# First layer's memory attention: transposes two steps behind the scores, eleven steps, first maximum alone ahead of the gate

## The reference, cut to what matters

```python
h = rmsnorm(x, g_mix[0])
mem_k, mem_v = split(rmsnorm(mem, g_mem) @ w_mem_kv[0])     # 256 memory rows, 4 heads of 64
p = h @ w_in_a[0]
u, q_mem = p[..., :2 * 768], p[..., 2 * 768:]
a, gate = split(u + b_glu)
v = causal_dwconv(a * sigmoid(gate), w_dw_a, b_dw_a)        # 768 channels, width 31
mix = silu(layernorm(v))
logits = einsum("bshd,bmhd->bhsm", q_mem, mem_k) / 8        # memory attention
mem_o = einsum("bhsm,bmhd->bshd", softmax(logits), mem_v)
x = x + concatenate([mix, mem_o]) @ w_out[0]
```

## Time and profile before

| | |
|---|---|
| median of 3 runs | 1653.23 us (1648.83 to 1654.64) |
| profiled execution, its own time | 1653.36 us |
| its span, first to last instruction | 1651.6 us |
| granted TensorE clock, mean | 0.996 |
| PE busy | 1605.1 us, 97% |
| DVE busy | 883.3 us, 53% |
| ACT busy | 733.1 us, 44% |
| POOL busy | 714.2 us, 43% |

### The profile page before, as it was taken

How to read it: one execution, slowest core, us unless ns; L and a number is a source line. 1 busy time by engine, 2 the same in 40 slices (tenths; PEclk the granted TensorE clock), 3 DMA queues, 4 the chain that set the end, 5 groups by cost and what they waited for, 6 DMA issues and landing times.

```text
span 1651.6 us, 23637 instructions
## 1 busy us (share of the span) xinstructions
PE 1605.1 (97%) x8452; PEld 1270.7 (77%) x8452; DVE 883.3 (53%) x1451; ACT 733.1 (44%) x1157; POOL 714.2 (43%) x406
## 2 busy tenths in 40 slices
PE   8899999999999999999999999999999999999998
PEld 7656788888888887666888888888887777887776
DVE  7887545445521124434366666611286654587654
ACT  6433544444432235444455555533335643535532
POOL 4433334444445444443444444454435542445431
PEclk9999999999999999999999999999999999999999
DMA  7212133323333332111223233333422443324441
GB/s 255 65 52 65 53 101 102 99 89 91 102 113 102 103 103 71 47 50 39 90 90 102 90 90 100 102 115 112 136 77 81 135 135 109 121 65 131 126 139 51
DMA packets 52972, 161.01 MB, mean 97 GB/s; under 512 B 8736, under 2 KB 8864, under 8 KB 52896
## 3 DMA queue, kind: packets, MB, share of 16 engines
q1 hardware_dynamic: 51744, 156.31, 30.9%
q10 hardware_dynamic: 1152, 3.67, 0.7%
HBM read 141.08 MB, written 2.10 MB: 87 GB/s over the span
## 4 chain that ended last, share of the span: by engine, by line
PE 85%; DVE 10%; ACT 2%; issue 2%; DMA 0%; POOL 0%; DVEq 0%; SPq 0%; ACTq 0%; POOLq 0%
PE banks L1886 23%; PE banks L1888 23%; PE banks L1887 23%; PE banks L2445 2%; PE banks L1932 2%; PE banks L1933 2%; PE banks L1934 2%; PE banks L2161 1%; PE banks L2073 1%; PE banks L2108 1%; DVE roped L1678 1%; PE banks L2091 1%; DVE chain L1497 1%; DVE pt_c L1724 1%; PE banks L2068 1%
## 5 line engine op out<-in xcount | busy, mean ns | idle before, releaser
L651 POOL TENSOR_TENSOR w_lo<-raw,w_hi 128x1024 fp32r<-128x1024 f32 x252 | 610.1, 2430 | 700.4 <-ACT w_hi L734 700.2
L1886 PE MATMUL banks<-xs_hi,w_hi 128*128 128x512 f32 (+2 forms) x1488 | 590.7, 397 | 5.1 <-DVE xs_lo L1559 1.6
L1888 PE MATMUL banks<-xs_hi,w_lo 128*128 128x512 f32 (+2 forms) x1488 | 577.5, 388 | 0.0
L1887 PE MATMUL banks<-xs_lo,w_hi 128*128 128x512 f32 (+2 forms) x1488 | 576.6, 388 | 0.0
L734 ACT ACTIVATE w_hi<-raw 128x1024 fp32r<-128x1024 f32 x255 | 263.8, 1052 | 235.8 <-PE banks L1888 204.6
L1886 PEld LDWEIGHTS banks<-xs_hi,w_hi 128*128 128x128 f32 x1488 | 280.2, 188 | 74.4 <-issue 19.0
L1888 PEld LDWEIGHTS banks<-xs_hi,w_lo 128*128 128x128 f32 x1488 | 280.0, 188 | 57.8
L1887 PEld LDWEIGHTS banks<-xs_lo,w_hi 128*128 128x128 f32 x1488 | 280.6, 189 | 52.3 <-issue 0.5
L1886 PE MATMUL banks<-hid_hi,w_hi 128*128 128x512 f32 x352 | 136.9, 389 | 0.0
L1887 PE MATMUL banks<-hid_lo,w_hi 128*128 128x512 f32 x352 | 136.9, 389 | 0.0
L1888 PE MATMUL banks<-hid_hi,w_lo 128*128 128x512 f32 x352 | 136.9, 389 | 0.0
(11 more groups left out here) (273 smaller groups left out, 2018.9 us busy)
## 6 DMA issues: line engine op xcount, KB each, us to landing
raw<-wstream SPq DMA_DIRECT2D x255, 512.0 KB, 3.5
swap_c<-prob_c SPq DMA_DIRECT2D x256, 64.0 KB, 2.0
x<-xT SPq DMA_DIRECT2D x4, 512.0 KB, 9.7
out<-pt SPq DMA_DIRECT2D x8, 256.0 KB, 2.0
memx<-memT SPq DMA_DIRECT2D x4, 256.0 KB, 5.1
ws_sb<-wsT ACTq DMA_DIRECT2D x2, 512.0 KB, 4.6
rope_sb<-rope ACTq DMA_DIRECT2D x2, 512.0 KB, 6.1
qk<-post_rows ACTq DMA_DIRECT2D x2, 512.0 KB, 5.0
```

The source lines that it names most:

```text
L651: nc.gpsimd.tensor_tensor(w_lo[s][:].rearrange("p k c -> p (k c)"), raw[s][:], w_hi[s][:].rearrange("p k c -> p (k c)").bitcast(f32), SUB) ...
L1886: MM(dst, w_hi[slot][:, k, :], hi, start=start, stop=False)
L1887: MM(dst, w_hi[slot][:, k, :], lo, start=False, stop=False)
L1888: return MM(dst, w_lo[slot][:, k, :], hi, start=False, stop=stop)
```

## The change

The table gets eleven steps in place of ten: (2,0), (2,3), (2,7), (3,3), (3,7), (4,3), (4,7), (5,3), (5,7), (6,3), (6,7). At step i PE issues the scores of block i and the transposes of block i-2, DVE and ACT copy block i-2 down. The outputs stand at steps 6 and 10. Ahead of the gate product DVE now issues only the maximum and the reciprocal of block 0; all other maxima and reciprocals stand in their steps. `pair_ended` is no longer called. No instruction is added or dropped; the second output stays at (6,7).

```diff
--- before.py
+++ after.py
@@ -72,7 +72,7 @@
 IN2_UNITS = DFF // P
 ATT_FIRST = 9
 STEP = 6
-A_AT = [divmod(16 + 39 * i // 9, KT) for i in range(10)]
+A_AT = [divmod(16 + 39 * i // 10, KT) for i in range(11)]
 B_AT = [(3 + i, 4) for i in range(8)]
 B_AT += [divmod(11 * KT + 40 * p // 3 + q, KT) for p in range(MT) for q in (0, 3, 6, 10)]
 B_LATE = 7
@@ -932,8 +932,8 @@
                     for i in a_steps(j, k):
                         if 0 < i < att_m0.n:
                             exponentials(att_m0, i)
-                        if 1 <= i <= att_m0.n:
-                            odd_down(att_m0, i - 1)
+                        if 2 <= i <= att_m0.n + 1:
+                            odd_down(att_m0, i - 2)
             gate_sigmoid(MT - 1)
             high_for(U_MEM1)
             for p in range(2):
@@ -1506,32 +1506,25 @@
 
             for j in range(2 * MT):
                 t = j // 2 - 1
-                ahead = a_steps(j, 0) + a_steps(j, 1) if j in (2, 4) else []
-                for i in ahead:
-                    maxima(att_m0, i)
-                    if i == 0:
-                        inverses(att_m0, 0)
-                        maxima(att_m0, 1)
-                        even_down(att_m0, 0)
+                if j == 2:
+                    maxima(att_m0, 0)
+                    inverses(att_m0, 0)
                 if j >= 2 and j % 2 == 0:
                     own.wait()
                     glu_product(t)
                 for k in range(KT):
                     at = KT * (j % 2) + k
                     for i in a_steps(j, k):
-                        if 1 < i < att_m0.n and i not in ahead:
+                        if 0 < i < att_m0.n:
                             maxima(att_m0, i)
-                        if 1 < i <= att_m0.n:
-                            even_down(att_m0, i - 1)
-                        if 1 < i < att_m0.n:
+                        if 2 <= i <= att_m0.n + 1:
+                            even_down(att_m0, i - 2)
+                        if 0 < i < att_m0.n:
                             inverses(att_m0, i)
-                        p = pair_ended(i)
-                        if p is not None:
-                            mem_out_down(p)
+                        if i in (QT + 2, 2 * QT + 2):
+                            mem_out_down(i // QT - 1)
                     if t >= 0:
                         conv_taps(t, at, at + 1)
-                    if (j, k) == (2, 2):
-                        inverses(att_m0, 1)
                 if 8 <= j < 12:
                     conv_finish(j - 8)
                 scaled(glu[:, j // 2, CW - 1:] if j % 2 == 0 else gate[j // 2 % 2][:], U_GLU + j,
@@ -2206,13 +2199,12 @@
                     if i == 0:
                         pe.wait_ge(acc_free, U_GLU)
                     scores(att_m0, i)
-                p = pair_ended(i)
-                if p is not None:
-                    output(att_m0, p)
-                if i == 1:
+                if i in (QT + 2, 2 * QT + 2):
+                    output(att_m0, i // QT - 1)
+                if i == 2:
                     pe.wait_ge(vt_down, VT_M0 + 2)
-                if 1 <= i <= att_m0.n:
-                    transposes(att_m0, i - 1)
+                if 2 <= i <= att_m0.n + 1:
+                    transposes(att_m0, i - 2)
 
             def ln_rows(dst, src, tiles):
 
```

## The result

The changed kernel takes 1660.38 us in the median of 5 runs (1658.22 to 1661.25), the kernel before 1653.23 (1648.83 to 1654.64, 5 runs). The ratio is 1.0042, with a 95% interval of 1.0029 to 1.0054: slower by about 7 us, and between 5 and 9. The profiled execution took 1659.49, its span is 1657.7 (before: 1653.36 and 1651.6).

The account below looks back on a forecast made before the run. DVE's path through the attention was taken as the bound up to its last copy, which lets `conv_parts` start. Terms summed to 5.06 us later, 1653.36 to 1658.4 us; full range 1654.5 to 1661.0, the forecast's own 1656.5 to 1660.3.

Parts of the forecast that it names:

- (a): First gate product and block 1: product starts only 0.17 earlier, block 1 then needs a whole uncovered step, +1.60 us.
- (c): Second gate product: with step 4 ahead of it, DVE waits for ACT's chain up to the sigmoid, +2.64 us.
- (d): POOL's low parts of the weights hold DVE taps with two SBUF inputs: units 3, 4, 5 cost +0.33, +0.04, +0.44 us.
- (e): From unit 5 on: one copy more stands alone, +0.34 us; the third gate product waits less, -0.33 us.
- Does DVE wait for PE after the change?: Tightest at block 6: PE's scores, output and transposes, 3.1 us, against DVE's 3.25 ahead of its copy; no wait, 0.
- Rival 1: PE's waits in the attention stretch decide, those for scaled probabilities go: faster, 1650.8 us; chance 0.10.
- Rival 2: ACT is ready for the second sigmoid, so that product costs 0 to 0.9: 1655.8 to 1656.7 us; chance 0.14.
- rival 3: POOL's low parts meet other DVE taps: 1655.2 us if only `banks`, 1660.1 if both whole; chance 0.12.
- Rival 4: The end hangs on something other than DVE's last copy and stays: 1653.4 us; chance 0.04.

Follow-up runs that it names:

- e1_gate2: Changed kernel with step 4 back at (4,1) and block 4's maximum ahead of the second gate product: ratio 1.0039, first maximum to `conv_parts` 55.32 us.
- e2_head: Changed kernel with block 1's maximum back ahead of the first gate product, its reciprocal behind tap 2: ratio 1.0022, first maximum to `conv_parts` 56.30 us.
- e4_busy: Changed kernel plus twelve PE products that nobody reads, ahead of block 6's scores: ratio 1.0033, first maximum to `conv_parts` 55.66 us.
- e8_both_busy: e3_both plus sixteen PE products that nobody reads, ahead of block 5's scores: first maximum to `conv_parts` 52.02 us, single execution.
- e10_swap4: Changed kernel with ACT's sigmoid ahead of the weights' high part in unit 4: first maximum to `conv_parts` 58.65 us, single execution.
- e5_lag: Kernel before with only the lag of two, its own early places and maxima kept, two late steps: ratio 1.0007, first maximum to `conv_parts` 54.66 us.
- e6_cover: Kernel before with DVE's convolution tap moved between copy and reciprocal from block 2 on: ratio 1.0007, first maximum to `conv_parts` 49.58 us.
- e7_lag_cover: Kernel before with only the lag of two, and DVE's tap moved ahead of the reciprocal: ratio 1.0001, first maximum to `conv_parts` 52.56 us.
- e3_both: Changed kernel with early maxima of blocks 1 and 4 back and step 4 at (4,1): ratio 1.0021, first maximum to `conv_parts` 53.53 us.
- e11_busy2: Changed kernel plus unread PE products, nine ahead of block 2's scores and twelve ahead of block 6's: first maximum to `conv_parts` 55.70 us, single execution.

## Why the prediction was right, and where not

The time, 1660.38, is in the range (1654.5 to 1661.0), at its upper end, and just above the forecast's own (1656.5 to 1660.3). The direction was right.

| step | forecast | profile after |
|---|---|---|
| (a) block 1's step (55.98 - 47.73, against 54.87 - 48.25) | +1.60 | +1.63 |
| (c) second gate product (75.96 - 70.85 = 5.11, against 2.45) | +2.64 | +2.66 |
| (d) low part of unit 3: 62.38 to 64.84 less a tap 0.66, against 1.49 | +0.33 | +0.31 |
| (d) low part of unit 4: product 76.89 - 75.96, against 0.78 | +0.04 | +0.15 |
| (d) low part of unit 5: 1.26, against 0.88 | +0.44 | +0.38 |
| (e) one copy alone | +0.34 | +0.34 |
| (e) third gate product | -0.33 | -0.34 |
| DVE's wait for PE at block 4's copy (86.48 - 83.11, against 1.85) | 0 | **+1.52** |
| sum | 5.06 | 6.65 |
| last copy less first maximum (56.32, against 49.64) | | 6.68 |

(a) and (c) are shown by taking them back: the wait of 2.58 goes to 0.26 in `e1_gate2`, the one of 1.09 goes in `e2_head`. What each would give the stretch alone can't be read from these two, as PE's waits and the clock moved with each edit. Both together can be, from the two runs in which the clock costs DVE nothing (the second a single execution): 55.66 in `e4_busy` less 52.02 in `e8_both_busy` is 3.64, and 4.55 without the 0.91 that only the second has, against 4.29 in the table. In every trace taps with two SBUF inputs that overlap POOL's low part take 1.6 to 2.6 us instead of 0.74, and the low parts' places decided how much; `e10_swap4` moved a low part, and the instruction that it then overlapped was held.

The step that failed is "Does DVE wait for PE after the change? [...] No wait, by little." It set scores, output and transposes, 3.1 us, against 3.25 of DVE. From the scores at 80.39 to the end of the transposes at 85.0 it took 4.6, because the output ran at half clock. The step also looked at DVE's copy alone: ACT's exponentials of block 6 wait for the same transposes, which the lag of two brings into their step, and it is by them that the whole 1.52 reaches DVE. At full clock both waits are nothing (`e4_busy`), by the little that the forecast said. The durations in that step had been taken from a stretch in which PE never waited longer than 1.7 us, and the forecast itself said that PE's waits for exponentials would grow. `e4_busy` shows the term and its cause: 1.55 us come back when PE has work in its wait. So the time lies in the range because the range was wide enough for a term that the forecast had put at nothing.

Rival 1 (PE decides) fell: PE's 2.6 us went and nothing was gained. Rival 2 fell by the wait of 2.58, rival 3 by the low parts, which met the taps that were named, near 63 and near 89. Rival 4 fell with `conv_parts` at 104.94.

Open: from the median to the median it is 7.15 us, in the profiled spans 6.1. The difference is within the interval. Single executions of one kernel differ by more than that (1649.75 to 1655.89 in 22 of before), and the traces differ far behind the change by a fall of the clock more or less of 1.5 to 1.8 us (`e5_lag`, `e6_cover`, `e7_lag_cover`: 1551.3, 1554.6, 1551.1 us behind the stretch). The traces of before and after have three such falls each behind the stretch, those of `e5_lag` and `e7_lag_cover` two, that of `e6_cover` four. Whether a change here alters how often that happens wasn't tried.

## What to carry to other kernels

Follow the chain, then the order of the engine that it runs on: here 4.3 of the 6.7 us were lost by moving two instructions of DVE out of times in which it had to wait for ACT anyway. The lag took a wait from an engine off the chain and won nothing, while PE's idle time came to lie in longer pieces. On PE such a piece can have a price of its own, so where a change lengthens one, cost the work behind it at half clock as one end of the range. And a lag of one more step uses up the slack of a tile with two buffers: ask who now waits for its release in the same step.

## What the runs showed of the hardware

- An idle PE ahead of dense work was followed by a granted clock of 0.50 for 3.4 us (behind waits of 2.73 and 3.69 us after the change, 4.71 in `e1_gate2` and `e3_both`) or for 6.8 us (3.40 in `e5_lag`, 3.92 in `e7_lag_cover`, 4.26 in `e10_swap4`), each inside a stretch that ran at 1.00. More work on PE made the stretch shorter (`e4_busy`, 2.9 us added, 1.55 won).
- The same wait can be followed by a fall or not. Ahead of block 2's scores PE idles 2.74 us in `e4_busy` and in `e1_gate2`, which do the same up to there; in the first the clock was at half from 56.4 to 59.8, in the second it stayed at 1.00 until 75.4. PE's rows, `e4_busy` first; its scores take 1.23 instead of 0.70:

```profile
56.44 1.23 PE L2066 MATMUL banks<-mem_kv,qm 64*128 64x256 f32 x4 [2.74 <-ACT prob L809]
```

```profile
56.33 0.70 PE L2069 MATMUL banks<-mem_kv,qm 64*128 64x256 f32 x4 [2.74 <-ACT prob L810]
```

- A fall was free where PE was ahead of DVE: `e4_busy` has one from 56.4 to 59.8, `e11_busy2` one from 68.6 to 72.0, DVE waits for PE behind neither, and the stretches are 55.66 and 55.70.
- A DVE instruction with one SBUF input and an SBUF output (`TENSOR_SCALAR chain<-glu`, 0.48 us) was held by POOL's low part to 2.12 us as well in `e10_swap4`, while the one that writes PSUM just ahead of it took 0.75. The Trainium skill, "SBUF — State Buffer", section "Who interferes with whom", names `tensor_scalar` in its two-port mode among what can contend with GpSimd for the shared pair of ports. The trace agrees in that the instruction was held; that it ran in this mode no row says.
